# Strassen's scheme for the last projection of a two-block transformer step on one Trainium2 core

## The reference

```python
def rmsnorm(x, g):
    xf = x.astype(jnp.float32)
    y = xf * lax.rsqrt(jnp.mean(xf * xf, axis=-1, keepdims=True) + EPS)
    return (y * g.astype(jnp.float32)).astype(x.dtype)

def swiglu_ffn(h, w_ffn_in, w_ffn_out):
    gate, up = jnp.split(h @ w_ffn_in, 2, axis=-1)
    return (jax.nn.silu(gate) * up) @ w_ffn_out

# end of second_block
        h = rmsnorm(x, pre_ffn_g[l]) * (1.0 + sc2) + sh2
        y = swiglu_ffn(h, w_ffn_in[l], w_ffn_out[l])
        x = x + ga2 * rmsnorm(y, post_ffn_g[l])
```

## Time and profile before

| | |
|---|---|
| median of 3 runs | 1348.56 us (1347.37 to 1348.98) |
| span of the profiled execution | 1346.8 us |
| PE busy over the span | 1327.9 us (99%) |
| DVE busy | 901.4 us (67%) |
| ACT busy | 526.4 us (39%) |
| GpSimd busy | 83.8 us (6%) |
| granted clock of TensorE, mean | 1.000 |
| read from HBM, written | 171.26 MB, 4.20 MB |

### The profile page before, as it was taken

One profiled execution on the slowest core, in us unless ns is written; L12 is line 12 of the kernel. 1 busy time (PEld: TensorE's weight loads), 2 busy tenths in 40 slices (PEclk: granted clock), 3 DMA queues, 4 the chain that ended last, 5 costly groups with the idle time before them and its releaser, 6 DMA issues.

```text
span 1346.8 us, 15738 instructions
## 1 busy us (share of the span) xinstructions
PE 1327.9 (99%) x6461; PEld 1077.6 (80%) x6461; DVE 901.4 (67%) x1126; ACT 526.4 (39%) x747; POOL 83.8 (6%) x148
## 2 busy tenths in 40 slices
PE   7999999999999999999999999999999999999998
PEld 4799688778888888887888777778878888888886
DVE  4787878988777777678758899766875433332224
ACT  4552444344334443222422666774333222222112
POOL 0000001000000001010000100000002220000000
PEclk9999999999999999999999999999999999999999
DMA  9543046324445555654123211112224332224331
GB/s 390 191 141 126 17 155 220 125 78 175 163 162 196 171 183 186 217 202 173 71 94 98 90 64 63 63 63 96 98 86 131 116 115 94 94 98 161 107 104 63
DMA packets 32887, 176.47 MB, mean 131 GB/s; under 512 B 4128, under 2 KB 4400, under 8 KB 17840
## 3 DMA queue, kind: packets, MB, share of 16 engines
q1 hardware_dynamic: 19440, 128.78, 26.7%
q0 software_dynamic: 13376, 46.69, 10.8%
HBM read 171.26 MB, written 4.20 MB: 130 GB/s over the span
## 4 chain that ended last, share of the span: by engine, by line
PE 90%; DVE 5%; issue 2%; ACT 2%; DMA 2%; SPq 0%; DVEq 0%; ACTq 0%
PE bank L1475 27%; PE bank L1477 26%; PE bank L1476 26%; PE bank L1814 2%; PE bank L1815 2%; PE bank L1820 2%; PE bank L1680 1%; DMA adaf<-ada 1%; PE bank L2010 1%; PE bank L1980 1%; DVE WL L830 1%; DVE sums L1174 1%; PE bank L1998 1%; PE bank L1997 1%; DMA raw<-weights 1%
## 5 line engine op out<-in xcount | busy, mean ns | idle before, releaser
L1475 PE MATMUL bank<-hH,WH 128*128 128x512 f32 x992 | 390.1, 393 | 0.9 <-DVE WL L830 0.6
L830 DVE TENSOR_TENSOR WL<-raw,WH 128x2048 fp32r<-128x2048 f32 x103 | 234.5, 2278 | 230.2 <-ACT WH L372 230.2
L1477 PE MATMUL bank<-hH,WL 128*128 128x512 f32 x992 | 386.4, 390 | 0.0
L1476 PE MATMUL bank<-hL,WH 128*128 128x512 f32 x992 | 386.2, 389 | 0.0
L372 ACT ACTIVATE WH<-raw 128x2048 fp32r<-128x2048 f32 x106 | 201.5, 1904 | 237.3 <-DMA raw<-weights 237.3
L1475 PEld LDWEIGHTS bank<-hH,WH 128*128 128x128 f32 x992 | 186.3, 188 | 42.6 <-issue 3.3
L1477 PEld LDWEIGHTS bank<-hH,WL 128*128 128x128 f32 x992 | 186.2, 188 | 39.6
L1476 PEld LDWEIGHTS bank<-hL,WH 128*128 128x128 f32 x992 | 186.3, 188 | 37.6 <-issue 0.2
L859 DVE SCALAR_TENSOR_TENSOR ada_acc<-ada_half,csil,ada_acc 128x1024 f32<-128x1024 f32 x70 | 89.7, 1281 | 6.4 <-DMA ada_half<-ada_later 3.8
L1307 DVE SCALAR_TENSOR_TENSOR cacc<-uT,vec,cacc 128x511 f32<-128x511 f32 (+29 forms) x120 | 83.3, 755 | 0.0
L335 POOL DMA_DIRECT2D ada_half<-ada_later x80 | 42.4, 530 | 571.8 <-DVE ada_acc L859 333.4
(11 more groups left out here) (333 smaller groups left out, 2075.1 us busy)
## 6 DMA issues: line engine op xcount, KB each, us to landing
raw<-weights SPq DMA_DIRECT2D x108, 1024.0 KB, 4.9
ada_half<-ada_later POOLq DMA_DIRECT2D x80, 512.0 KB, 4.4
adaf<-ada SPq DMA_DIRECT2D x8, 1024.0 KB, 19.8
xT<-x_t SPq DMA_DIRECT2D x4, 512.0 KB, 5.7
x_rows<-xB POOLq DMA_DIRECT2D x32, 64.0 KB, 2.2
x_tok<-x_rows POOLq DMA_DIRECT2D x1, 2048.0 KB, 10.9
out_t<-x_tok SPq DMA_DIRECT2D x8, 256.0 KB, 2.0
ctxT<-ctx_t SPq DMA_DIRECT2D x1, 1024.0 KB, 28.6
```

What stands on the lines that cost most here:

```text
L830: TT_(WL[:, slot, 0:width], raw[:, slot, 0:width], WH[:, slot, 0:width], sub).then_inc(s.lo_done, 1)
L1475: mm(o, lh, rh, start=start, stop=False, skip_group_check=skip)
L1476: mm(o, lh, rl, start=False, stop=False, skip_group_check=skip)
L1477: return mm(o, ll, rh, start=False, stop=stop, skip_group_check=skip)
```

## The change

The last projection is done by one level of Strassen's scheme. The output is cut in two halves of 256 tokens and two halves of 512 columns, the depth in pairs of neighbouring tiles (the two of a chunk), which are the two halves of the depth. Instead of 8 products of quarter size per pair there are 7. They are made in two passes over the depth: in pass one (chunks `C_DOWN2` to `C_REST` - 1) four products per chunk, 24 matmuls, and in pass two (from `C_REST`, the same 11 chunks loaded again) three products per chunk, 18 matmuls. Pass two adds on into banks that pass one has used, so between the passes ACT copies six banks to `parts` (`keep`); `copied` tells PE when. The last three chunks are interleaved.

The sums of weight blocks are made by GpSimd in place in `raw` (`weight_sums`): per chunk of pass one two additions of 512 columns, of pass two one of 512 and one of 1024. `split_hi` then waits for `w_sum` instead of the load. In pass two only 1536 columns are split. The sums of activations are made by DVE in the up stage, per pair, and kept with the activations in `gF` (7 combinations of 256 tokens); four are split there (`pair_lo`), the other three during the last projection (`rest_hi` on ACT, `rest_lo` on DVE). From chunk `C_DOWN2` + 2 on there are four slots (`RING4`, `slot_of`), the load of c then waits for chunk c - 4. The load of `x_tok` moves from the start of the stage to the end of its fourth chunk, behind the sums of six chunks on GpSimd's queue. At the end DVE combines banks and `parts` (`combine`, and the additions of the tail), GpSimd multiplies four half tiles by the gain, and the token tiles are finished in the order 2, 3, 0, 1. Several semaphores are merged into others to stay within their number.

```diff
@@ SP
-                if c >= SLOTS:
-                    sp.wait_ge(s.mm_done, 16 * (c - SLOTS + 1))
-                sp.dma_start(raw[:, c % SLOTS, :], weights[c]).then_inc(raw_in[c % SLOTS], 16)
+                sp.wait_ge(s.mm_done, 16 * (c - (SLOTS if c <= RING4 else SLOTS + 1) + 1))
+                sp.dma_start(raw_of(c), weights[c if c < C_REST else c - PAIRED]).then_inc(raw_in[slot_of(c)], 16)
@@ GpSimd
-            pool.wait_ge(s.mm_done, 16 * C_DOWN2)
+            def weight_sums(c):
+
+                pool.wait_ge(raw_in[slot_of(c)], 16 * loads_up_to(c))
+                a11, a21 = raw_of(c, CW * W_A11, CW * W_A11 + CW), raw_of(c, CW * W_A21, CW * W_A21 + CW)
+                a12, a22 = raw_of(c, CW * W_A12, CW * W_A12 + CW), raw_of(c, CW * W_A22, CW * W_A22 + CW)
+                if c < C_REST:
+                    nc.gpsimd.tensor_tensor(a21, a21, a22, add).then_inc(s.w_sum, 1)
+                    nc.gpsimd.tensor_tensor(a12, a11, a22, sub).then_inc(s.w_sum, 1)
+                else:
+                    nc.gpsimd.tensor_tensor(a21, a21, a11, add).then_inc(s.w_sum, 1)
+                    pool.wait_ge(s.w_sum, 2 * (c - C_DOWN2) + 1)
+                    nc.gpsimd.tensor_tensor(quarters(c, 0, 3, 2), quarters(c, 0, 3, 2), quarters(c, 2, 4), add).then_inc(s.w_sum, 1)
+
+            for i in range(6):
+                weight_sums(C_DOWN2 + i)
+            pool.wait_ge(s.mm_done, 16 * (C_DOWN2 + 4))
             pool.dma_start(x_tok[:, :, :], x_rows.rearrange("(t p) c -> p t c", p=P)).then_inc(s.rows_in, 16)
+
+            for i in range(6, 2 * PAIRED):
+                weight_sums(C_DOWN2 + i)
@@ ACT
+            def keep(n, banks, t, half):
+
+                act.wait_ge(s.y_done, n)
+                for x in range(2):
+                    A(piece(parts, t + x, half), bank[banks + x][:, :], ACT.Copy).then_inc(s.copied, 1)
+
+            for i in range(2 * PAIRED - 2):
+                if i == PAIRED + 1:
+                    keep(1, 6, 2, 1)
+                    keep(2, 2, 0, 0)
+                    keep(3, 4, 0, 1)
+                split_hi(C_DOWN2 + i + 2, split_width(C_DOWN2 + i + 2))
+                if 2 <= i < PAIRED + 2:
+                    rest_hi(i - 2)
@@ DVE
+            for i in range(2 * PAIRED - 2):
+                c = C_DOWN2 + i + 2
+                if 2 <= i < PAIRED + 2:
+                    rest_lo(i - 2)
+                if PAIRED + 2 <= i:
+                    combine(i - PAIRED - 2)
+                split_lo(c, split_width(c))
+            for x in range(2):
+                dve.wait_ge(s.y_done, 3 + x + 1)
+                TT_(piece(parts, 2 + x, 1), bank[4 + x][:, :], piece(parts, 2 + x, 1), sub).then_inc(s.row_ready, 1)
+            for x in range(2):
+                dve.wait_ge(s.y_done, 3 + 3 + x)
+                TT_(piece(gained, 2 + x, 0), bank[2 + x][:, :], gpB[:, first_half], mult).then_inc(s.y_scaled, 1)
+                TT_(piece(parts, x, 0), bank[2 + x][:, :], piece(parts, x, 0), add).then_inc(s.row_ready, 1)
+                row_bias(2 + x, 3 + x)
+            last_add(2, 0)
+            for x in range(2):
+                dve.wait_ge(s.row_ready, 5 + x)
+                dve.wait_ge(s.y_done, 3 + 5 + x)
+                TT_(piece(parts, x, 0), bank[6 + x][:, :], piece(parts, x, 0), sub).then_inc(s.row_ready, 1)
+                dve.wait_ge(s.row_ready, 7 + x)
+                TT_(piece(gained, x, 0), piece(parts, x, 0), gpB[:, first_half], mult).then_inc(s.y_scaled, 1)
+                if x == 0:
+                    last_add(3, 1)
+                last_add(x, 2 + x)
@@ PE
+            for q in range(PAIRED):
+                c, first, last = C_DOWN2 + q, q == 0, q == PAIRED - 1
+                have(c)
+                pe.wait_ge(s.ffn_lo, FT + q + 1)
+                for at, block, to, freed in ((T_SUM, W_A12, 6, 0), (T_HIGH, W_A11, 2, FT - 2), (T_LOW, W_A21, 4, FT - 1),
+                                             (T_DIFF, W_A22, 0, FT)):
+                    if first and freed:
+                        pe.wait_ge(s.bank_free, B_UP2 + 2 * freed)
+                    ins = product(c, q, at, 0, block, to, (0, 1), first, last)
+                    if last and to:
+                        ins.then_inc(s.y_done, 1)
+                ins.then_inc(s.mm_done, 16)
+            for q in range(PAIRED - 3):
+                have(C_REST + q)
+                pe.wait_ge(s.ffn_lo, FT + PAIRED + q + 1)
+                if q == 0:
+                    pe.wait_ge(s.copied, GATE_COPIES + 4)
+                last_column(q)
+                row2(q)
+                if q == 0:
+                    pe.wait_ge(s.copied, GATE_COPIES + 6)
+                row1(q, q == 0).then_inc(s.mm_done, 16)
+            e, f, g = range(PAIRED - 3, PAIRED)
+            have(C_REST + e)
+            pe.wait_ge(s.ffn_lo, FT + 2 * PAIRED)
+            row1(e)
+            have(C_REST + f)
+            row1(f)
+            last_column(e)
+            last_column(f)
+            row2(e)
+            have(C_REST + g)
```

More of the change, by code:

```diff
@@ L48 @@
 C_DOWN2 = C_UP2 + FT
[L49 removed]
+PAIRED = FT // 2
+C_REST = C_DOWN2 + PAIRED
+N_CHUNKS, N_LOADS = C_REST, C_REST + PAIRED
 ADA_FIRST = 8
@@ L82, with slot_of, loads_up_to @@
 SLOTS = 3
+RING4 = C_DOWN2 + 2
+def slot_of(c):
+    return c % SLOTS if c < RING4 else (0, 3, 1, 2)[(c - RING4) % 4]
+def loads_up_to(c):
+    return sum(slot_of(x) == slot_of(c) for x in range(c + 1))
+assert [slot_of(RING4 - x) for x in (3, 2, 1)] == [0, 1, 2]
+PAIR_W = HALF_L = 256
+T_SUM, T_LOW, T_DIFF, T_HIGH, T_LAST, T_ROW1, T_ROW2 = range(7)
+W_A11, W_A21, W_A12, W_A22 = range(4)
+GATE_COPIES = 16
+BIAS_AT, GAIN_AT = (1, 2, 4, 6), (7, 8, 3, 5)
 Y_BANKS = {0: (2, 3, 0, 1), 1: (2, 3, 0, 1), 2: (0, 1, 2, 3), 3: (2, 3, 0, 1)}
@@ L807, in _, with rest_hi @@
             pin_ln_exp()
[L808 to L818, removed]
+            def rest_hi(q):
+                act.wait_ge(s.mm_done, 16 * (C_DOWN2 + q) + 16)
+                A(gH[:, q, 0:3, :], gF[q][:, 4:7, :], ACT.Copy).then_inc(s.ffn_hi, 1)
@@ new lines, in row_square @@
+            def row_square(n, t, half, src):
+                if n >= 2:
+                    act.wait_ge(s.yy_ready, 3 * KT + n - 1)
+                A(scratch[:, n % 2, :], src, ACT.Square, accum_out=ysum[:, 2 * t + half:2 * t + half + 1])                    .then_inc(s.yy_ready, 1)
+            for t in range(TT):
+                act.wait_ge(s.row_ready, t + 1)
+                row_square(t, t, 1, piece(parts, t, 1))
+            for n, t in enumerate((2, 3, 0, 1)):
+                if t >= 2:
+                    act.wait_ge(s.row_ready, t + 3)
+                    row_square(TT + n, t, 0, bank[t][:, :])
+                else:
+                    act.wait_ge(s.row_ready, 7 + t)
+                    row_square(TT + n, t, 0, piece(parts, t, 0))
+                act.wait_ge(s.yy_ready, 3 * KT + 5 + n)
+                act.wait_ge(s.y_scaled, 3 * KT + BIAS_AT[t])
+                own.link(A(yscale[:, t:t + 1], ysum[:, 2 * t:2 * t + 1], ACT.Ln, bias=ybias[:, t:t + 1], scale=1.0 / D))
+                A(yscale[:, t:t + 1], yscale[:, t:t + 1], ACT.Exp, scale=-0.5).then_inc(s.root_ready, 1)
@@ L2049, in _ @@
                     project(bank[2 * (t % 3) + x][:, :], C_UP2 + t, x, hH, hL, ALL).then_inc(s.mm_done, step(x, 2))
-            def rows(q, t, half, first, last):
-                at = slice(P * t, P * t + P)
-                o = bank[2 * t + half][:, :]
-                for kk in range(2):
-                    k, ws = 2 * q + kk, slice(D * kk + CW * half, D * kk + CW * half + CW)
-                    slot = (C_DOWN2 + q) % SLOTS
-                    wh, wl = WH[:, slot, ws], WL[:, slot, ws]
-                    ins = mm3(o, GH[:, k, at], GL[:, k, at], wh, wl, first and kk == 0, last and kk == 1)
-                return ins
@@ L2062, in _ @@
-            Q = FT // 2
-            for q in range(Q - 2):
-                have(C_DOWN2 + q)
-                pe.wait_ge(s.ffn_lo, FT + 2 * q + 2)
-                for t in (3, 1, 2, 0):
-                    if q == 0 and t < 3:
-                        pe.wait_ge(s.bank_free, B_UP2 + 2 * (FT, FT - 2, FT - 1)[t])
-                    for half in range(2):
-                        ins = rows(q, t, half, q == 0, False)
-                ins.then_inc(s.mm_done, 16)
-            have(C_DOWN2 + Q - 1)
@@ L2080, in tiles @@
+            for x in range(2):
+                row2(f, (x,))
+                row2(g, (x,), True).then_inc(s.y_done, 1)
 def tiles(w, cols):
```

183 lines of the change are left out of this document (126 added, 57 removed).

## The result

The changed kernel takes 1367.33 us (median of 4 runs, 1366.79 to 1370.26) against 1348.24 of the kernel before; the ratio is 1.0139, 95% interval 1.0125 to 1.0153. Slower by 19 us, forecast 1364.0. The profiled execution has a span of 1365.6 us, 18.8 more than before.

The account below looks back on a forecast made before the run. The last projection was taken as bound by its number of matmuls alone. -15.0 + 3.0 + 9.2 + 1.6 + 10.7 + 5.9 = +15.4 us gave a forecast of 1364.0 us, range 1351 to 1370.

Parts of the forecast that it names:

- 66 matmuls fewer: Last projection: 462 instead of 528 matmuls at 0.2267 us each, -15.0 us.
- stalls and clock of pass one: Pass one: late chunks, no slack in a slot's round and the x_tok load there, +3.0 us (0.8 to 6).
- gap between the passes: PE waits for four ACT copies queued behind a late chunk's high part, +9.2 us; 7.6 with nothing waiting for the shared read.
- pass two, stalls and clock: Pass two: the shared read sets the pace, 10.7 us lost (6 to 15), plus 1.6 for one clock restart.
- tail: After the last matmul: DVE ends 8.8 us later instead of 2.9, +5.9 us (4 to 7).
- the line from two narrow rows: GpSimd's addition price, extended from 128 and 256 columns: 1.14 us for 512 columns, 2.22 for 1024.
- the walk: Step-by-step timeline of the last projection from the start of pass one, giving stalls, clock and tail.
- The lock: GpSimd's reads and DVE instructions with two SBUF inputs exclude each other; holds 5.25 of 5.44 us, then 4.98 of 4.08.
- The 0.14 us: A two-input instruction that had to wait for the other engine then needs 0.14 us less than usual.
- The clock: One fall to half clock, in the long stall between the passes, costing 1.6 us at the restart.
- D+2: Third chunk of the last projection, D being the first: ready at 12.3 us, wanted at 10.9, 1.5 lost.
- The rival without a lock: GpSimd and DVE run side by side in the last projection: +3.4 us, 1352.0 us, chance 15%.

Follow-up runs that it names:

- the run with fills: Changed kernel with GpSimd filling the weight slot with a constant, as long as the additions alone but without reading SBUF: 1353.85 us against 1367.33.
- c1_busy_between: Changed kernel with eight matmuls of zeros added onto bank 0 between the passes, so TensorE works while ACT copies: 1365.64 us against 1367.33.
- a1_copies_early: Changed kernel with ACT's six bank copies one chunk earlier in its queue: 1361.50 us against 1367.33.
- a4_dve_sums2: Changed kernel with the weight sums of pass two made by DVE, those of pass one still by GpSimd: 1359.26 us against 1367.33.
- b1_again: Second run of the changed kernel with pass-two sums made ahead in the up stage, stored in HBM, and copies two chunks earlier: 1344.49 us.
- t1_tail_only: Changed kernel with token tile 2 scaled by ACT and added by GpSimd, DVE adding the other three after combining all banks: 1367.22 us.
- b1_staged_sums: Changed kernel with pass-two sums made ahead by DVE in the up stage, stored in HBM, and ACT's copies two chunks earlier: 1343.91 us.

## Why the prediction was right

The time lies 3.3 us above the forecast and inside the range. Term by term, from the profiled executions ("rest" is what waits and clock leave over; a part of it is that a matmul before a wait is counted with its whole duration of 0.39 us and not with the distance of 0.2267):

| term | forecast | measured |
|---|---|---|
| 66 matmuls fewer | -15.0 | -15.0 (462, pitch 0.2267 at full clock) |
| stalls and clock of pass one | +3.0 | +5.8 (65.66 for 59.85): 2.9 idle, 1.7 clock, 1.2 rest |
| gap between the passes | +9.2 | +8.5 |
| pass two, stalls and clock | +10.7 and 1.6 | +14.0 (58.85 for 44.9): 7.3 idle, 5.7 clock, 1.0 rest |
| tail | +5.9 | +5.2 |
| stage begins later | 0 | +0.4 |
| sum | +15.4 | +18.9 |

- The saving came whole. The price per matmul from the distance of starts held.
- GpSimd's price by the line from two narrow rows held for an addition that had to wait: 1.14 and 2.22 in the walk, 1.16 and 2.24 in the rows. One that starts at once takes more, 1.30 and 2.36.
- The lock held, to 0.02 us in the rows above, and the run with fills shows that it is the reading, at a cost of 12 to 14 us. The 0.14 us that the walk takes off a DVE instruction after a wait does not follow from the row it stands beside (0.53 for 0.73 is 0.20 less); here it came out all the same, 1.09 for 1.22.
- The gap between the passes held, with its cause (released by ACT's copies) and with its two sizes, 8.5 with the lock and 7.65 without.
- The clock was mis-sized: one fall of 1.6 was in the sum, four with 7.4 us came. The step that failed is that only the long stall between the passes would bring one; the single fall on which it rests came 4 us after the last matmul. The waits at which the clock fell in the changed kernel were 2.44, 8.52, 3.15 and 2.47 us long. The Trainium skill, TensorE: Matmul & The Clock Gate, section "HAM oscillation", tells of a kernel whose clock falls again at each of its waits for operands, of about 3 to 5 us. The trace agrees that such a fall comes back with each long wait, and shows it at shorter ones too, 2.44 and 2.47 us.
- Pass two's idle time was over-sized (10.7 for 7.3). That a slower PE leaves GpSimd and DVE more time per chunk would make this the same error as the clock's. It isn't shown: in c1_busy_between the first fall of pass two is gone, and PE's waits there are 7.38 us for 7.34. The reason stays open, and that an idle time 3.4 us too long and a clock 5.8 us too cheap partly cancel is luck.
- D+2 late by 1.5: it was 2.44. The subtraction of the last pair (1.71 us for 1.22) and that of D+2 both met GpSimd's additions.
- The tail held in size for the changed kernel. As to cause, DVE's queue is what ends last, but taking two additions off it gained 0.8 us of DVE's time and nothing of the kernel's. So the claim that the tail is DVE's work alone isn't shown: lock and output transfers seem to stand right behind it.
- The rival without a lock (1352.0) is what the run with fills is near to (1353.85).

## What to carry to other kernels

Fewer matmuls pay only if the ways that feed them fit into the shorter period: count for each engine, and for each pair of engines that shut each other out, the work per chunk against the new time per chunk, and a slot's whole round against the number of slots. Additions moved to GpSimd beside DVE instructions with two SBUF inputs add to DVE's time, as if they were on DVE and at half the pace (1.30 us for 0.69, 2.36 for 1.22); they belong where the stage has slack, if need be with a trip through HBM. When waits of TensorE are summed, a fall of the clock should be charged with each long one: here it cost 1.6 to 2.5 us each time, and it came with most waits of 2.3 us and more.

## What the runs showed that was not expected

- The length of a wait doesn't settle whether the clock falls. It fell around waits of PE of 2.00 us (a1_copies_early), 2.28 (a4_dve_sums2), 2.41 (b1_again), 2.44 and 2.47 (changed), but not around 1.99 (t1_tail_only), 2.33 (b1_staged_sums) and 2.45 (c1_busy_between); all but 2.47 and 1.99 stand at the same place, chunk D+2. It can fall when work has been going on again: the gap of the changed kernel ended at 1235.51, the low clock began at 1236.35 and lasted 3.4 us.
- Matmuls of ones with a moving operand of zeros kept the granted clock at 1.0 (2.4 GHz) for 7.13 us (c1_busy_between).
- GpSimd's fills of 2048 columns (1.81 us each) ran beside DVE's subtractions without a trace of delay in either: 1814 and 1810 ns for the two fills, 2286 for a subtraction of 2048 columns.
